# Two-layer attention trunk: value products for one head at a time, with the values' high and low halves side by side as stationary operand

## Chip, core and metric

The kernel runs on one core of one Trainium2 chip. The metric is device time in microseconds (us) for one execution. An engine here is TensorE (PE, its weight loads are PEld), VectorE (DVE), ScalarE (ACT), GpSimd (POOL) or the queue of SyncE (SP).

## What is computed

Two layers of a trunk over 544 tokens: 512 prompt tokens and 32 sample tokens that also see 1024 cached positions. The part that matters here:

```python
h = rmsnorm(x, g_pre_mix)
q, k, v, q_mla, ckv, k_rope, gate_a, gate_b = split(h @ w_in)
# branch A, 8 heads x 64, strictly causal, stick-breaking weights
z = einsum('bqhd,bkhd->bhqk', q, k) * SB_SCALE
a = where(visible, exp(log_sigmoid(z) + suffix_sum(log_sigmoid(-z))), 0)
o_sb = einsum('bhqk,bkhd->bqhd', a, v)
# branch B, 8 heads, latent attention, softmax over chunk-causal scores
p = softmax(where(visible, s, -inf));  o_mla = (p @ c_kv) @ w_uv
mix = (sigmoid(gate_a)*(o_sb @ w_proj_sb) + sigmoid(gate_b)*(o_mla @ w_proj_mla)) @ w_out
# then ConvFFN (w_up, causal conv, gelu, w_down) and a per-layer embedding
```

All is float32. A product of two float32 matrices is made as three products of rounded parts: each operand is split into a high part (fp32r) and a low part (what is left), and `PARTS = ((0,0),(0,1),(1,0))` multiplies high by high, high by low and low by high.

## The kernel before, in words

Activations lie transposed (features on partitions, 544 tokens in the free dimension). TensorE has a fixed, hand-written order. After a few opening projections each layer runs 37 **steps**, s = 0 to 36. Step s belongs to unit s: `("s", t, qb)` is query block qb (128 queries) of head pair t in branch A, `("m", t, qb)` the same in branch B, and S and M are units of the sample tokens. The order is: pairs s0, s1, unit S, pairs s2, s3, unit S, pairs m0 to m3, two units M. So a pair's four units start at step 0, 4, 9, 13, 18, 22, 26 and 30; this start is `start(br, t)`.

In step s TensorE does, in this order: scores of unit s (`sb_scores` L1610 and L1613, or `ml_scores` L1744 and L1750) into the PSUM banks 4 to 7; the tiles of `AHEAD` for this step (the value products `pv`, L1691 and L1695); `turn(s-1)`, which transposes the attention weights of the unit before (L1653, for samples L1643 and L1645); small tiles of `AFTER` (`vt`, `kv`, `ot` and others); and then from one to four quarters of projection tiles from `FILL` (L1536, twelve matmuls of 272 columns a quarter).

ScalarE and VectorE go through the same steps in their own fixed orders. ScalarE: sigmoids (L820, L825) or, after the scores' maxima, exponents (L839); evacuation of AHEAD tiles (L736); `weights_hi(s-1)` (L862); evacuation of AFTER and FILL tiles. VectorE: scans (L1231) or maxima (L1266, L1268); evacuation of AHEAD tiles; `weights_lo(s-1)`; `products(s)` (L1252) or `normalise(s)` (L1284), for which turn(s) waits; the rest. The scores of unit s wait until weights_lo(s-2) is done. All low parts go through one helper, `lo`, recorded as L1074.

Transposed weights of one pair lie in `at`, a single buffer. Before the change a pair's value products are two tiles: `pva` for query blocks 0 and 1 in step start+3, `pvb` for blocks 2 and 3 in step start+5. Each takes the values of both heads (128 columns) as stationary operand and the weights of both heads as moving one, so half of each output, where a head's values meet the other head's weights, is not read.

Tiles other than scores live in PSUM banks 0 to 3. A planner that runs when the program is built goes through the order of events, gives each tile one bank (`pv`, `ot`, `sv`, `zt`, ...) or a pair of banks (projections, `kv`, `vt`), and notes in `BEFORE` which tile had the bank last. `banks_free(t)` makes TensorE wait until the readers of that tile have counted up. For a value product the last reader is VectorE.

GpSimd splits each streamed weight chunk into its parts (L600, L606), in a ring of four slots; SP loads a chunk when the chunk four places before it has been used.

Of the kernel before, what the change touches and what calls it, by code (L numbers as in the profile page):

```python
# [110 lines left out]
def build(nc, x_in, p_in, wstream, vec, kc, vc, cct, cc, krc, consts, trig,  # L111
          y_out, k_out, v_out, c_out, kr_out, conv_out):
    top = ExitStack()
    with top:
# [59 lines left out]
        at = reg(b1, 2, 2, ATW)  # L174
# [3 lines left out]
        v_s = reg(b2, 2, 2, QB, P)  # L178
# [3 lines left out]
        vm = reg(b3, 2, 2, QB, P)  # L182
# [117 lines left out]
        AHEAD = {start(br, t) + d: [("pv" + h + br, t)] for br in "sm" for t in range(PAIRS) for h, d in (("a", 3), ("b", 5))}  # L300
# [124 lines left out]
        def released(c):  # L425
# [3 lines left out]
            if c in CACHES:  # L429
# [13 lines left out]
                 "z_done w_done b_done r_done a_done at_tr at_hi at_lo "  # L443
# [6 lines left out]
        with ExitStack() as st:  # L450
# [160 lines left out]
            def _(act):  # L611
# [16 lines left out]
                for layer in range(DEPTH):  # L628
# [101 lines left out]
                    def pv_tile(t):  # L730
                        act.wait_ge(S["p_done"], AT[t] + 1)
                        if t[0] == "pvas" and t[1] == 2:
                            act.wait_ge(pre["qr_in"], QR_MOVES * (layer + 1))
                        o, q = (o_sb if t[0][3] == "s" else o_ml), slice(0, SEQ // 2) if t[0][2] == "a" else slice(SEQ // 2, SEQ)
# [15 lines left out]
                    def kv_tile(t):  # L750
                        act.wait_ge(S["p_done"], AT[t] + 1)
                        ac(kn[:, t[1] % 2, 0], bank(t), ACT.Copy)
                        ac(vm[:, t[1] % 2, 0], bank(t, 1).rearrange("p (b l) -> p b l", l=P),
                           ACT.Copy).then_inc(S["act_read"], 1)
# [88 lines left out]
                    def weights_hi(n):  # L843
                        br, t, qb = units[n]
                        act.wait_ge(S["at_tr"], n + 1)
                        if br == "S":
                            act.wait_ge(S["p_done"], AT[("pvbs", 2 * t + 1)] + 1)
                            ac(aT_s[0:DEC, 0, PAST:PAST + P], bank(tail(n))[0:DEC, 0:P], ACT.Copy).then_inc(S["act_read"], 1)
                            ac(wide(aT_s[:, 0, 0:PAST]), z_view(n, 512), ACT.Copy).then_inc(S["at_hi"], 1)
                            return  # L850
                        if br == "M":
                            if t == 0:
                                act.wait_ge(S["p_done"], AT[("pvbm", PAIRS - 1)] + 1)
# [4 lines left out]
                        if qb == 0 and units[n - 1][0] == "S":  # L858
                            act.wait_ge(S["p_done"], AT[("sv", units[n - 1][1])] + 1)
                        elif t > 0 and qb in (0, 2):  # L860
                            act.wait_ge(S["p_done"], AT[(("pva" if qb == 0 else "pvb") + br, t - 1)] + 1)
                        ac(at_view(0, qb), z_view(n, P * (qb + 1)), ACT.Copy).then_inc(S["at_hi"], 1)  # L862
# [180 lines left out]
            def _(dve):  # L1043
# [17 lines left out]
                for layer in range(DEPTH):  # L1061
# [98 lines left out]
                    def vt_tile(t):  # L1160
                        dve.wait_ge(S["act_read"], aread(t))
                        lo(v_s[:, t[1] % 2, 1], bank(t).rearrange("p (b l) -> p b l", l=P), v_s[:, t[1] % 2, 0], None)
                        lo(v_tail[0:DEC, 1, t[1]], bank(t, 1)[0:DEC, 0:P], v_tail[0:DEC, 0, t[1]], "dve_read")

                    def pv_tile(t):
                        dve.wait_ge(S["act_read"], aread(t))
                        o, q = (o_sb if t[0][3] == "s" else o_ml), slice(0, SEQ // 2) if t[0][2] == "a" else slice(SEQ // 2, SEQ)
# [119 lines left out]
                    def weights_lo(n):  # L1287
# [207 lines left out]
            def _(pe):  # L1495
# [3 lines left out]
                for layer in range(DEPTH):  # L1499
# [135 lines left out]
                    def turn(n):  # L1635
# [443 lines left out]
```

## Time and profile before

| | |
|---|---|
| median of 3 runs | 1863.4 us (1861.43 to 1866.7) |
| the profiled execution, its own time | 1863.8 us |
| its span, first to last instruction | 1862.0 us |
| PE busy | 98% of the span |
| DVE, ACT, POOL busy | 49%, 30%, 58% |
| attention steps of layer 0 | about 43 to 310 us |
| attention steps of layer 1 | about 968 to 1235 us |

Busy time of PE is a union of pipelined matmuls, so the start of one matmul to the start of the next is the better measure of what one costs. "Idle" in a row is the engine's idle time just before the first instruction of that row, with what ended it.

### The profile page before, as it was taken

How to read it: one execution, taken by the hardware profiler on the slowest of the kernel's cores; microseconds unless marked ns; L12 is line 12 of the kernel's file. 1: busy time of each engine (PE TensorE's matmuls, PEld its weight loads, DVE VectorE, ACT ScalarE, POOL GpSimd, SP SyncE). 2: the span in 40 equal slices, each digit the busy share in tenths (PEclk: the TensorE clock that was granted, in tenths of full speed). 3: DMA queues.
4: the chain of work that ended last, by engine and by line, in shares of the span. 5: the costliest groups of instructions: out<-in, count | busy, mean ns of one | idle time of the engine just before them, and what ended most of it. 6: DMA issues, size and time to landing. Idle time of an engine off the chain costs nothing.

```text
span 1862.0 us, 33695 instructions
## 1 busy us (share of the span) xinstructions
PE 1832.2 (98%) x14262; PEld 1775.2 (95%) x14262; DVE 920.4 (49%) x1570; ACT 557.7 (30%) x1165; POOL 1073.5 (58%) x994
## 2 busy tenths in 40 slices
PE   9999999999999999999999999999999999999999
PEld 8989889999999999999999898899999999999999
DVE  6666675332755532523656666752237555225143
ACT  4434443112422221202334344431134222122021
POOL 8685534656555555556666854346465555555564
PEclk9999999999999999999999999999999999999999
DMA  5242111333222222223242421122422222222222
GB/s 187 87 130 75 64 41 59 112 99 133 69 91 89 82 91 91 87 78 100 95 146 89 126 74 58 48 78 86 142 94 69 91 84 87 91 91 82 84 88 94
DMA packets 76230, 170.48 MB, mean 92 GB/s; under 512 B 6384, under 2 KB 34160, under 8 KB 76080
## 3 DMA queue, kind: packets, MB, share of 16 engines
q1 hardware_dynamic: 68752, 160.79, 26.9%
q10 hardware_dynamic: 7328, 7.54, 1.3%
q8 instruction: 113, 1.85, 0.4%
q14 instruction: 37, 0.30, 0.0%
HBM read 156.41 MB, written 9.79 MB: 89 GB/s over the span
## 4 chain that ended last, share of the span: by engine, by line
PE 85%; DVE 6%; POOL 3%; ACT 3%; DMA 1%; issue 1%; SPq 0%; DVEq 0%; ACTq 0%; POOLq 0%
PE ps L1536 72%; PE ps L1571 2%; PE ps L1695 2%; POOL wsp L606 2%; PE ps L1653 2%; DVE xT L1408 1%; DVE xn L1074 1%; POOL wsp L600 1%; DVE mix L1405 1%; DVE R L1074 1%; DMA raw<-in_wstream 1%; ACT ps L839 1%; PE ps L1610 1%; PE ps L1744 1%; ACT R L862 1%
## 5 line engine op out<-in xcount | busy, mean ns | idle before, releaser
L1536 PE MATMUL ps<-xn,wsp 128*128 128x272 f32 x7824 | 1003.4, 289 | 9.2 <-POOL wsp L606 5.3
L1536 PEld LDWEIGHTS ps<-xn,wsp 128*128 128x128 f32 x7824 | 986.7, 189 | 13.2 <-issue 9.6
L606 POOL TENSOR_TENSOR wsp<-raw,wsp 128x256 fp32r<-128x256 f32 (+1 forms) x578 | 723.3, 1274 | 22.3
L600 POOL CAST wsp<-raw 128x512 fp32r<-128x512 f32 (+2 forms) x372 | 325.5, 890 | 662.4 <-DMA raw<-in_wstream 567.8
L1536 PE MATMUL ps<-R,wsp 128*128 128x272 f32 x3840 | 486.2, 288 | 0.1
L1536 PEld LDWEIGHTS ps<-R,wsp 128*128 128x128 f32 x3840 | 482.7, 189 | 1.3 <-DVE xT L1103 0.5
L1074 DVE SCALAR_TENSOR_TENSOR R<-ps,R 64x256 fp32r<-64x256 f32 (+8 forms) x232 | 127.8, 560 | 85.1 <-ACT R L674 27.9
L1424 DVE TENSOR_TENSOR mix<-ps,rstd 128x272 f32<-128x272 f32 x88 | 38.8, 441 | 202.6 <-PE ps L1536 192.2
L959 ACT ACTIVATE mix<-vv 128x2 f32<-128x2 f32 x88 | 17.9, 204 | 363.0 <-DVE mix L1426 363.0
L1074 DVE SCALAR_TENSOR_TENSOR R<-mix,R 128x544 fp32r<-128x544 f32 (+2 forms) x86 | 74.5, 867 | 81.3 <-ACT R L980 66.9
L1432 DVE SCALAR_TENSOR_TENSOR ps<-mix,vv,ps 128x546 f32<-128x546 f32 x88 | 69.4, 789 | 55.6 <-ACT ps L968 55.6
L1571 PE MATMUL ps<-xn,wsp 128*128 128x272 f32 x576 | 80.3, 295 | 6.8 <-DVE xn L1074 6.8
L1571 PEld LDWEIGHTS ps<-xn,wsp 128*128 128x128 f32 x576 | 74.5, 189 | 10.9 <-DVE xn L1074 9.8
L1471 DVE TENSOR_TENSOR A<-ps,A 128x544 f32<-128x544 f32 x32 | 23.2, 724 | 109.3 <-PE ps L1536 109.3
L1231 DVE TENSOR_TENSOR_SCAN xT<-xT 128x128 f32<-128x128 f32 (+3 forms) x64 | 62.1, 1011 | 20.2 <-ACT xT L820 20.2
L968 ACT ACTIVATE ps<-mix,vv 128x546 f32<-128x546 f32 x88 | 71.4, 812 | 1.6 <-DVE mix L1426 1.6
L1434 DVE SCALAR_TENSOR_TENSOR ps<-mix,vv,ps 128x546 f32<-128x546 f32 x88 | 69.6, 791 | 3.1
L1088 DVE TENSOR_TENSOR acc<-acc,mix 128x544 f32<-128x544 f32 x30 | 32.7, 1089 | 64.9 <-ACT mix L649 64.9
L862 ACT ACTIVATE R<-ps 128x256 fp32r<-128x256 f32 (+1 forms) x64 | 45.2, 707 | 46.9 <-PE ps L1653 46.2
L649 ACT ACTIVATE mix<-A 128x544 f32<-128x544 f32 x16 | 10.6, 661 | 150.4 <-DVE A L1471 150.4
L1695 PE MATMUL ps<-R 128*128 128x512 f32 x192 | 52.3, 407 | 0.6 <-issue 0.4
L1653 PE MATMUL ps<-con,xT 128*128 128x128 f32 x320 | 46.9, 277 | 4.2 <-DVE xT L1284 2.5
(228 smaller groups left out, 1441.3 us busy)
## 6 DMA issues: line engine op xcount, KB each, us to landing
raw<-in_wstream SPq DMA_DIRECT2D x233, 512.0 KB, 3.5
raw<-in_wstream SPq DMA_DIRECT2D x48, 128.0 KB, 2.6
raw<-in_wstream SPq DMA_DIRECT2D x16, 384.0 KB, 3.0
raw<-in_kc SPq DMA_DIRECT2D x8, 512.0 KB, 3.6
raw<-in_vc SPq DMA_DIRECT2D x8, 512.0 KB, 4.3
xT<-in_x_in SPq DMA_DIRECT2D x8, 272.0 KB, 4.8
out_k_out<-mix ACTq DMA_DIRECT2D x8, 272.0 KB, 2.9
xT<-in_x_in SPq DMA_DIRECT2D x1, 2176.0 KB, 9.3
```

Of the source, the lines that this page charges most:

```text
L600: ins = nc.gpsimd.tensor_copy(dst[:, 0, f], part[:, f])
L606: ins = nc.gpsimd.tensor_tensor(dst[:, 1, f], part[:, f], dst[:, 0, f].bitcast(F32), ALU.subtract)
L862: ac(at_view(0, qb), z_view(n, P * (qb + 1)), ACT.Copy).then_inc(S["at_hi"], 1)
L968: ac(uc[v], e[:, 0:T + 2], ACT.Identity, scale=vv[:, V_CW + f:V_CW + f + 1], bias=vv[:, V_CB + f:V_CB + f + 1]).then_inc(S["conv0"], 1)
L1074: ins = v.scalar_tensor_tensor(dst, src, scale, hi.bitcast(F32), ALU.mult, ALU.subtract)
L1231: v.tensor_tensor_scan(x, x, x, 1.0, ALU.mult, ALU.min).then_inc(S["r_done"], 1)
L1432: link(v.scalar_tensor_tensor(uc[w], uext[w][:, 1:T + 3], vv[:, V_CW + 2 * FT + f:V_CW + 2 * FT + f + 1], uc[w], ALU.mult, ALU.add))
L1434: v.scalar_tensor_tensor(uc[w], uext[w][:, 2:T + 4], vv[:, V_CW + 4 * FT + f:V_CW + 4 * FT + f + 1], uc[w], ALU.mult, ALU.add).then_inc(S[ ...
L1536: mm = pe.matmul(z[:, h], w[:, x, (k0 + k) * P:(k0 + k + 1) * P], rhs[:, y, k, h * HT:(h + 1) * HT], start=(k == 0 and (x, y) == (0, 0)), ...
L1571: mm = pe.matmul(z[:, h], w[:, x, k * P:(k + 1) * P], xn[:, y, k, h * HT:(h + 1) * HT], start=(k == 0 and (x, y) == (0, 0)), stop=(k == KT ...
L1653: mm = pe.transpose(ps[:, ZB + 2 * (n % 2) + r, kb * P:(kb + 1) * P], x[:, r, kb * P:(kb + 1) * P], ident)
L1695: mm = pe.matmul(z.rearrange("p r (b q) -> p r b q", b=2), val[:, x, kb], a[:, :, :, kb * P:(kb + 1) * P], start=(kb == 0 and i == 0), sto ...
```

## The change

Value products are made head by head. For head r of a pair the stationary operand is 64 columns of the values' high part beside 64 columns of the low part; the moving operand is the weights' high part and then their low part. One tile covers all four query blocks: key block kb meets the queries from block kb on, (4-kb)*128 columns. Rows 0 to 63 of the output are high values' products and rows 64 to 127 those of the low values; VectorE adds the halves when it evacuates. Both tiles of a pair, `pv0` and `pv1`, stand in step start+5; step start+3 has none. The weights' buffer and the values' buffers are laid out anew, transposes of head 0 are written in reversed block order, and head 1's output has its query blocks reversed until evacuation.

```diff
-        AHEAD = {start(br, t) + d: [("pv" + h + br, t)] for br in "sm" for t in range(PAIRS) for h, d in (("a", 3), ("b", 5))}
+        AHEAD = {start(br, t) + 5: [("pv0" + br, t), ("pv1" + br, t)] for br in "sm" for t in range(PAIRS)}
...
+        PV_AT = {t: n for n, t in enumerate([t for s in range(STEPS) for t in ahead(s) if t[0][0:2] == "pv"])}
...
         def at_view(x, qb):
-            o = qb * (qb + 1) // 2 * P
-            return at[:, x, :, o:o + P * (qb + 1)]
+            a = at[:, x, qb * P:(qb + 1) * P]
+            return bass.AP(tensor=a.tensor, offset=a.offset,
+                           ap=[a.ap[0], [(2 * ATW // P - 1 - 5 * qb) * P, 2], [3 * P, qb + 1], [1, P]])
+        def at_keys(x, r, kb):
+            o = (2 * ATW // P - 4 - 3 * kb if r else 4 * kb) * P
+            return at[:, x, o:o + (QB - kb) * P]
...
                     def pv_tile(t):                      # ScalarE
+                        r = int(t[0][2])
                         act.wait_ge(S["p_done"], AT[t] + 1)
-                        for r in range(2):
-                            ins = ac(o[64 * r:64 * r + 64, 0, t[1], q], bank(t)[64 * r:64 * r + 64, 256 * r:256 * r + 256], ACT.Copy)
-                        ins.then_inc(S["act_read"], 1)
+                        z = turned(bank(t)[0:64], r)
+                        o = (o_sb if t[0][3] == "s" else o_ml)[64 * r:64 * r + 64, 0, t[1], 0:SEQ]
+                        ac(turned(o, 0), z, ACT.Copy).then_inc(S["act_read"], 1)
...
                     def pv_tile(t):                      # VectorE
                         dve.wait_ge(S["act_read"], aread(t))
-                        for r in range(2):
-                            lo(o[64 * r:64 * r + 64, 1, t[1], q], bank(t)[64 * r:64 * r + 64, 256 * r:256 * r + 256],
-                               o[64 * r:64 * r + 64, 0, t[1], q], "dve_read" if r else None)
+                        r, z = int(t[0][2]), bank(t)
+                        o = (o_sb if t[0][3] == "s" else o_ml)[64 * r:64 * r + 64, :, t[1], 0:SEQ]
+                        lo(turned(o[:, 1], 0), turned(z[0:64], r), turned(o[:, 0], 0), "pv_low")
+                        dve.wait_ge(S["pv_low"], PV_AT[t] + 1)
+                        v.tensor_tensor(turned(o[:, 1], 0), turned(z[64:128], r), turned(o[:, 1], 0).bitcast(F32),
+                                        ALU.add).then_inc(S["dve_read"], 1)
...
-                            lo(at_view(1, qb), z_view(n, P * (qb + 1)), at_view(0, qb), "at_lo")
+                            v.tensor_tensor(at_view(1, qb), z_blocks(n, qb), at_view(0, qb).bitcast(F32), ALU.subtract).then_inc(S["at_lo"], 1)
...
                     def pv(t):                           # TensorE
-                        pe.wait_ge(S["at_lo"], n + 1)
-                        z, blocks = bank(t).rearrange("p (r q) -> p r q", r=2), 2 if t[0][2] == "a" else QB
-                        for kb in range(blocks):
-                            for i, (x, y) in enumerate(PARTS):
-                                if kb == blocks - 1:
-                                    mm = pe.matmul(z[:, :, P:2 * P], val[:, x, kb], at[:, y, :, o + 2 * kb * P:o + (2 * kb + 1) * P],
-                                                   start=False, stop=(i == 2))
-                                else:
-                                    a = at[:, y, :, o:o + 2 * (blocks - 1) * P].rearrange("p r (b q) -> p r b q", b=2)
-                                    mm = pe.matmul(z.rearrange("p r (b q) -> p r b q", b=2), val[:, x, kb],
-                                                   a[:, :, :, kb * P:(kb + 1) * P], start=(kb == 0 and i == 0), stop=False)
+                        if r == 0:
+                            pe.wait_ge(S["dve_read"], dread(("vt" if br == "s" else "kv", p)))
+                            pe.wait_ge(S["at_lo"], start(br, p) + QB)
+                        for kb in range(QB):
+                            w = (QB - kb) * P
+                            z = bank(t)[:, 0:w] if r else bank(t)[:, 512 - w:512]
+                            for x in range(2):
+                                mm = pe.matmul(z, val[:, 2 * kb + r].rearrange("p x f -> p (x f)"), at_keys(x, r, kb),
+                                               start=(kb == 0 and x == 0), stop=(kb == QB - 1 and x == 1))
                         mm.then_inc(S["p_done"], 1)
```

The planner's code is unchanged; its banks follow from the new order of tiles.

## Rows read from the trace of the kernel before

**Rows 1.** The page's busy times.
```profile
PE 1832.2 (98%) x14262; PEld 1775.2 (95%) x14262; DVE 920.4 (49%) x1570; ACT 557.7 (30%) x1165; POOL 1073.5 (58%) x994
```
**Rows 2.** TensorE in order of time, pair s0: start, length, what, count.
```profile
67.72 0.94 PE L1695 MATMUL ps<-R 128*128 128x512 f32 x3
...
68.85 0.82 PE L1653 MATMUL ps<-con,xT 128*128 128x128 f32 x6
...
75.56 1.09 PE L1653 MATMUL ps<-con,xT 128*128 128x128 f32 x8 [0.28 <-DVE xT L1252]
```
**Rows 3.** VectorE in order of time, step 3.
```profile
72.55 1.82 DVE L1074 SCALAR_TENSOR_TENSOR R<-ps,R 64x256 fp32r<-64x256 f32 x3
```
**Rows 4.** TensorE in order of time: runs of one size, 512 and 128 columns.
```profile
105.81 2.89 PE L1625 MATMUL ps<-wsp,R 128*128 128x512 f32 x12
...
208.25 1.45 PE L1718 MATMUL ps<-R 128*128 128x128 f32 x12
```
**Rows 5.** Groups by line and shape: busy us, mean ns, idle before.
```profile
L1456 DVE TENSOR_TENSOR mix<-mix,ps 128x512 f32<-128x512 f32 x44 | 30.3, 688 | 5.0 <-ACT mix L991 0.6
...
L1088 DVE TENSOR_TENSOR acc<-acc,mix 128x544 f32<-128x544 f32 x30 | 32.7, 1089 | 64.9 <-ACT mix L649 64.9
...
L1074 DVE SCALAR_TENSOR_TENSOR R<-ps,R 64x256 fp32r<-64x256 f32 x64 | 26.8, 418 | 25.1 <-ACT R L736 24.7
L1074 DVE SCALAR_TENSOR_TENSOR R<-ps,R 128x512 fp32r<-128x512 f32 x40 | 26.0, 679 | 1.0 <-ACT vtail L724 0.6 <-ACT R L753 0.5
...
L862 ACT ACTIVATE R<-ps 128x512 fp32r<-128x512 f32 x16 | 9.6, 599 | 18.0 <-PE ps L1653 18.0
```
**Rows 6.** TensorE in order of time, steps 9 and 10 of layer 0.
```profile
115.26 2.32 PE L1695 MATMUL ps<-R 128*128 128x512 f32 x9
...
117.77 0.27 PE L1643 MATMUL ps<-con,xT 128*32 128x128 f32 x1
...
118.67 6.25 PE L1536 MATMUL ps<-xn,wsp 128*128 128x272 f32 x48
```
**Rows 7.** VectorE in order of time, step 9.
```profile
119.08 1.77 DVE L1231 TENSOR_TENSOR_SCAN xT<-xT 128x128 f32<-128x128 f32 x2
```
**Rows 8.** GpSimd in order of time, from step 8 of layer 0.
```profile
110.30 3.23 POOL L600 CAST wsp<-raw 128x512 fp32r<-128x512 f32 x2 [4.88 <-DMA raw<-in_wstream]
```
**Rows 9.** TensorE in order of time, step 10 of layer 0.
```profile
131.45 3.75 PE L1536 MATMUL ps<-xn,wsp 128*128 128x272 f32 x28 [1.92 <-POOL wsp L606]
```
**Rows 10.** TensorE in order of time, step 10 of layer 1.
```profile
1055.64 4.52 PE L1536 MATMUL ps<-xn,wsp 128*128 128x272 f32 x23 [2.16 <-POOL wsp L606]
```
**Rows 11.** Busy time by stretch there; the number before the DMA share is the granted clock.
```profile
1054.00:1056.00 2.00, 0.36 (x1) 0.39 (x2) 1.89 (x3) 0.00 (x0) 2.00 (x4) 0.84 0.91 228
```
**Rows 12.** TensorE and VectorE in order of time, step 14.
```profile
160.60 2.30 PE L1695 MATMUL ps<-R 128*128 128x512 f32 x9
...
161.56 1.27 DVE L1231 TENSOR_TENSOR_SCAN xT<-xT 128x256 f32<-128x256 f32 x2 [1.62 <-ACT xT L820]
```
**Rows 13.** TensorE, ScalarE and VectorE in order of time, step 25 and the turn after.
```profile
243.32 1.09 PE L1653 MATMUL ps<-con,xT 128*128 128x128 f32 x8 [0.50 <-DVE xT L1284]
...
240.00 0.75 ACT L839 ACTIVATE ps<-ps,small,rtok 128x512 f32<-128x512 f32 x1
...
238.78 0.23 DVE L1268 TENSOR_SCALAR small<-small,rtok 128x2 f32<-128x2 f32 x1
```
**Rows 14.** TensorE and VectorE in order of time, steps 27 and 28.
```profile
247.68 2.30 PE L1695 MATMUL ps<-R 128*128 128x512 f32 x9
...
252.55 0.62 PE L1744 MATMUL ps<-R,Ar 64*128 64x384 f32 x4 [0.49 <-DVE R L1074]
...
251.18 1.31 DVE L1074 SCALAR_TENSOR_TENSOR R<-ps,R 64x256 fp32r<-64x256 f32 x3 [2.28 <-ACT R L736]
```
**Rows 15.** TensorE in order of time, step 35.
```profile
298.53 2.31 PE L1695 MATMUL ps<-R 128*128 128x512 f32 x9
...
302.99 6.24 PE L1536 MATMUL ps<-xn,wsp 128*128 128x272 f32 x48 [0.81 <-ACT R L854]
```

More of the change, by code:

```diff
@@ L173, in build @@
         ATW = 10 * P
-        at = reg(b1, 2, 2, ATW)
+        at = reg(b1, 2, 2 * ATW)
         aT_s = reg(b1, 2, (CB + 1) * P)
@@ L177, in build @@
         b2 = b1 + 4 * ATW
-        v_s = reg(b2, 2, 2, QB, P)
+        v_s = reg(b2, 2, 2 * QB, 2, 64)
         kn = reg(b2, 2, 2, SEQ)
@@ L181, in build @@
         q_smp = reg(b3 + 2 * PAIRS * P, 2, PAIRS, P)
-        vm = reg(b3, 2, 2, QB, P)
+        vm = reg(b3, 2, 2 * QB, 2, 64)
         ol_s = reg(b3, 2, 2 * P)
@@ L239, in z_view, with z_blocks @@
             return ps[:, ZB + 2 * (n % 2):ZB + 2 * (n % 2) + 2, 0:w]
+        def z_blocks(n, qb):
+            return z_view(n, P * (qb + 1)).rearrange("p r (b q) -> p r b q", q=P)
         def bt_view(n, w):
@@ L254, in at_view, with turned, v_parts @@
         def at_view(x, qb):
-            o = qb * (qb + 1) // 2 * P
-            return at[:, x, :, o:o + P * (qb + 1)]
+            a = at[:, x, qb * P:(qb + 1) * P]
[4 more added lines that the diff above has]
+            return at[:, x, o:o + (QB - kb) * P]
+        def turned(ap, r):
+            z = ap.rearrange("p (b q) -> p b q", q=P)
+            return z[:, ::-1] if r else z
+        def v_parts(buf, i, y):
+            return buf[:, i, :, y]
         def backward(ap, n):
@@ L730, in pv_tile @@
                     def pv_tile(t):
+                        if t[0] == "pv0s" and t[1] == 2:
+                            act.wait_ge(pre["qr_in"], QR_MOVES * (layer + 1))
+                        r = int(t[0][2])
                         act.wait_ge(S["p_done"], AT[t] + 1)
-                        if t[0] == "pvas" and t[1] == 2:
-                            act.wait_ge(pre["qr_in"], QR_MOVES * (layer + 1))
-                        o, q = (o_sb if t[0][3] == "s" else o_ml), slice(0, SEQ // 2) if t[0][2] == "a" else slice(SEQ // 2, SEQ)
-                        for r in range(2):
-                            ins = ac(o[64 * r:64 * r + 64, 0, t[1], q], bank(t)[64 * r:64 * r + 64, 256 * r:256 * r + 256], ACT.Copy)
-                        ins.then_inc(S["act_read"], 1)
+                        z = turned(bank(t)[0:64], r)
+                        o = (o_sb if t[0][3] == "s" else o_ml)[64 * r:64 * r + 64, 0, t[1], 0:SEQ]
+                        ac(turned(o, 0), z, ACT.Copy).then_inc(S["act_read"], 1)
                     def qn_tile(t):
@@ L752, in kv_tile @@
                         ac(kn[:, t[1] % 2, 0], bank(t), ACT.Copy)
-                        ac(vm[:, t[1] % 2, 0], bank(t, 1).rearrange("p (b l) -> p b l", l=P),
+                        ac(v_parts(vm, t[1] % 2, 0), bank(t, 1).rearrange("p (b f) -> p b f", f=64),
                            ACT.Copy).then_inc(S["act_read"], 1)
@@ L859, in weights_hi @@
                             act.wait_ge(S["p_done"], AT[("sv", units[n - 1][1])] + 1)
-                        elif t > 0 and qb in (0, 2):
-                            act.wait_ge(S["p_done"], AT[(("pva" if qb == 0 else "pvb") + br, t - 1)] + 1)
-                        ac(at_view(0, qb), z_view(n, P * (qb + 1)), ACT.Copy).then_inc(S["at_hi"], 1)
+                        elif t > 0 and qb == 0:
+                            act.wait_ge(S["p_done"], AT[("pv1" + br, t - 1)] + 1)
+                        ac(at_view(0, qb), z_blocks(n, qb), ACT.Copy).then_inc(S["at_hi"], 1)
                     if layer > 0:
@@ L1161, in vt_tile @@
                         dve.wait_ge(S["act_read"], aread(t))
-                        lo(v_s[:, t[1] % 2, 1], bank(t).rearrange("p (b l) -> p b l", l=P), v_s[:, t[1] % 2, 0], None)
+                        lo(v_parts(v_s, t[1] % 2, 1), bank(t).rearrange("p (b f) -> p b f", f=64), v_parts(v_s, t[1] % 2, 0), None)
                         lo(v_tail[0:DEC, 1, t[1]], bank(t, 1)[0:DEC, 0:P], v_tail[0:DEC, 0, t[1]], "dve_read")
@@ L1178, in kv_tile @@
                         lo(kn[:, t[1] % 2, 1], bank(t), kn[:, t[1] % 2, 0], None)
-                        lo(vm[:, t[1] % 2, 1], bank(t, 1).rearrange("p (b l) -> p b l", l=P), vm[:, t[1] % 2, 0], "dve_read")
+                        lo(v_parts(vm, t[1] % 2, 1), bank(t, 1).rearrange("p (b f) -> p b f", f=64), v_parts(vm, t[1] % 2, 0), "dve_read")
                     def ql_tile(t):
@@ L1652, in turn @@
                             for kb in range(qb + 1):
-                                mm = pe.transpose(ps[:, ZB + 2 * (n % 2) + r, kb * P:(kb + 1) * P], x[:, r, kb * P:(kb + 1) * P], ident)
+                                j = qb - kb if r else kb
+                                mm = pe.transpose(ps[:, ZB + 2 * (n % 2) + r, j * P:(j + 1) * P], x[:, r, kb * P:(kb + 1) * P], ident)
                         mm.then_inc(S["at_tr"], 1)
```

15 lines of the change are left out of this document (6 added, 9 removed).

## The prediction

> **What bounds the kernel now.** I read the page first: PE is busy 98% of the span, the other engines at most 58% [rows 1]. So time leaves only if TensorE has less to do, or if a wait of TensorE goes or comes. Then TensorE's waits, and its order of time through the attention steps of layer 0: projection quarters cover most turns, and the stalls are 0.3 to 0.5 us each, at turns that come too early for VectorE [rows 2, 13, 14], one of 0.81 us for a PSUM bank [rows 15], and one for GpSimd's weights, 1.92 us in layer 0 at 131.45 us and 2.16 us in layer 1 [rows 9, 10]. Last I read ScalarE's and VectorE's order of time in each step that holds a value product, because these engines free the banks.
>
> **Matmul prices.** A matmul costs what lies from its start to the next one's. pva (three of 512 columns, three of 256) takes 68.85 - 67.72 = 1.13 us [rows 2]; pvb (nine and three) takes 117.77 - 115.26 = 2.51 [rows 6]. The six more make 1.38 us: 0.23 for 512. 272 columns are at most 6.25 / 48 = 0.13 [rows 6], so 256 some 0.12, and 0.08 is left for a group's start. 128 columns: nine transposes in 118.67 - 117.77 = 0.90 us, 0.10 to 0.11 [rows 6]; runs of twelve, with the tail of the last in them, give 0.24 and 0.12 as upper ends for 512 and 128 [rows 4]. No row shows 384 columns with 128 rows: between 0.12 and 0.23; halfway, 0.175, since from 256 to 512 the cost follows the columns.
>
> **What TensorE saves.** Before, a pair costs pva 68.85 - 67.72 = 1.13 us in step start+3 [rows 2] and pvb 2.51 us in step start+5. After, each head has two matmuls each of 512, 384, 256 and 128 columns: 0.46 + 0.35 + 0.24 + 0.21 = 1.26 us, so both 2.52, with the start 2.60 us (2.4 to 2.8 by the bounds for 384). All of this stands in start+5. So start+3 loses 1.13 us, start+5 gains 0.10. Over 16 pairs (4 pairs, 2 branches, 2 layers) that is 16.5 us, if nothing waits.
>
> **Start+3, does all of it count?** Turn(start+2) can come 1.13 us earlier: its weights come from the step before, and nothing stalls there. The next turn, start+3, stands in step start+4:
> - s0 and s2: it already waits 0.28 us for VectorE [rows 2], whose chain begins with scans after the k tile. That chain holds pva's two evacuations (the row of three has them and weights_lo), 2 * 0.418 less overlap = 0.8 us [rows 3, 5]. So 0.85 saved.
> - s1, s3, m3: a sample unit follows with long scores, no stall: 1.13 each.
> - m0 to m2: the turn waits for normalise, that for exponents, those for the maxima, whose end is 239.01 in step 25; exponents start at 240.00 after pva's evacuation and weights_hi [rows 13]. They can start 0.95 earlier, no more. So 0.97, 1.0, and 1.2 for m0, where a small bank wait goes too.
>
> Sum per layer: 2 * 0.85 + 3 * 1.13 + 3.17 = 8.3 us. Less 8 * 0.10 = 0.8.
>
> **What evacuation costs.** ScalarE: one copy of 512 a tile, 0.60 us. VectorE: `lo` 0.68 and an add of PSUM and SBUF 0.69 [rows 5], 1.39 a tile with the wait between; 64 partitions cost as much as 128, only the free size counts (a 64x256 `lo` takes 0.418 as above). Nothing shows an add whose halves and result lie on different partitions: from 0.69, as this add without a shift, up to 1.09, as the kernel's dearest add, of 544, both from SBUF [rows 5]; I take 0.69, the row with one operand in PSUM. Nor is the copy with a shift of partitions shown; 0.60 to 0.75, taken 0.60. With T as the start of pv0: pv0 is complete at T+1.5 and copied at T+2.15; pv1 complete at T+2.8 and copied at T+3.4. VectorE, free at F, gives pv0 back at max(F, T+2.15) + 1.4 and pv1 1.35 later. Before, one tile came back 1.5 us after its end. The subtraction in weights_lo costs the same as `lo`.
>
> **Banks: what TensorE now waits for.** I worked the planner's rule through the new order of tiles. In four steps the tile that TensorE opens right after the pair's turn gets a bank of pv0 or pv1, and waits for VectorE's adds:
> - Step 9 (s1): v3 opens banks 2 and 3, the last of them pv1's. Before, it opened 0 and 1 and didn't wait: turn(8) ends and L1536 starts at 118.67 [rows 6]. VectorE first has the rotation of qr1 and scans(9) until 119.08 + 1.77 = 120.85 [rows 7]. Then four instructions, 2.7 us: pv1 is free at 123.55. TensorE is there at T + 2.6 + 0.9 = 118.77. Stall 4.8 us. It replaces the stall of 1.92 (2.16) us that GpSimd causes one step later: GpSimd's unbroken run begins at 110.30 with a load [rows 8] that a tile of step 7 releases, so it isn't moved by the new stall. Net 2.9 us a layer.
> - Step 14 (s2): `ot` 0 gets pv0's bank. T is 160.60; VectorE's scans end at 162.83 [rows 12]; free at 164.25. TensorE is there at T + 2.6 + 0.2. Stall 0.8.
> - Step 18 (s3): ga1 gets pv1's bank. VectorE is idle when pv0 comes; free at T + 2.15 + 2.75 = T + 4.9; TensorE there at T + 3.5. Stall 1.4.
> - Step 35 (m3): gb3 gets both, free at T + 4.9 = 303.45 instead of 302.99, where it already stalls [rows 15]. 0.5.
>
> Elsewhere there is cover: in step 5, q2 opens 3.3 us after the pair's end, free 0.6 us before; in m0 to m2 the next user comes a step later. But in m1 and m2, steps 27 and 31, a single quarter covers VectorE: weights_lo ends at T + 5.2 instead of 251.18 + 1.31 = T + 4.8, and scores(28), which already waits 0.49 us for it [rows 14], goes with it: 0.3 less the 0.1 counted, 0.16 each, 0.3.
>
> VectorE loses nothing else: step 3, 7, 12 and 16 get lighter by 0.8 us each.
>
> Sum of waits per layer: 2.9 + 0.8 + 1.4 + 0.5 + 0.3 = 5.9 us.
>
> **The clock.** In layer 1 the granted clock fell behind TensorE's 2.16 us of idleness, to 0.84 in the mean of a 2 us stretch [rows 11], so to its lower level, 1.2 GHz, for part of it; the 23 matmuls that follow take 4.52 us, against 23 * 0.13 = 3.0 at the full 2.4 GHz [rows 6, 10]: 1.4 to 1.6 us. In layer 0 it didn't fall. A stall of 4.8 us in both layers should bring it both times, once more than before: 1.6 us.
>
> **Sum.** Per layer 8.3 - 0.8 - 5.9 = 1.6 saved, 3.2 for both, less 1.6 for the clock: 1.6. The profiled execution takes 1863.8 us (span 1862.0), so 1862.2; the runs' median is 0.4 below: **1861.8 us**.
>
> **Rivals.**
> - *A, no bank waits:* the banks come free in time (the planner gives others, or VectorE does the evacuation ahead of its scans). Then 8.3 - 0.8 - 0.3 = 7.2 a layer, 14.4: **1849 us**. For it: TensorE's own work does shrink by 16.5. Against: VectorE's order puts scans first [rows 7].
> - *B, half of the waits:* some of the four are covered, above all step 9: 1855 us.
> - *C, the add is dear (the other side):* at 1.09 us and not 0.69, each of pv0 and pv1 comes back 0.4 later. Step 9 loses 0.8, 14 0.4, 18 and 35 0.8 each, 27 and 31 0.8 each, step 5 a little: 4.6 a layer, 9.2 more: **1871 us**. It is slower by over 0.3% from an add of 1.0 us on. For it: nothing shows this shift of partitions. Against: adds of PSUM and SBUF take 0.69 in 44 cases [rows 5].
> - *D, wide matmuls don't pay by column:* if only the number of matmuls counted, 16 instead of 18 at 0.107, a pair would save 0.2 us and not 1.04: 13 us more, **1875 us**. Against: 512 columns cost 0.23 us and 128 about half of that [rows 4, 6]. A page speaks for a mild form of D: the Trainium skill, "TensorE: Matmul & The Clock Gate", section "Back-to-back issue gap", gives about 131 ns for 512 columns and 81 ns for 128 in a stream of weight loads and matmuls. By it a pair would fall from about 2.16 to 1.70 us, an estimate from that page, so the sum would be some 9 us higher than mine. The trace disagrees: 0.23 and 0.10 us.
>
> **Chances and range.** My forecast 0.62 (its own range 1857 to 1866: each of ten stalls is off by some tenths), A 0.14, B 0.10, C 0.11, D 0.03. A measurement of this kernel can tell 0.3%, 5.6 us. Faster than 1857.8: A, most of B, and a tenth of my case: 0.28. Slower than 1869.0: C, D: 0.12. Within: 0.60. The range, 1850 to 1869, leaves out D, most of C and half of A.
>
> **What would show it.** L1695 and L1691 become one line with 256 matmuls, about 2.6 us a pair; no value product in steps 3, 7, 12, 16; VectorE's `lo` of 64x512 and an add after it, 0.7 us each, 32 of each; an idle time of 4.8 us before L1536 in step 9, ended by VectorE's add, and none, or little, for GpSimd in step 10; 0.8 before `ot`, 1.4 before ga1, 1.3 before gb3; a lower clock behind step 9 in both layers. I am wrong if the stall in step 9 is short, if the add isn't 0.7, or if waits show up that I called covered (q2 in step 5, scores in steps 23 and 24).

## The result

The changed kernel takes 1866.7 us (median of 18 runs, 1864.4 to 1868.0) against 1862.6 for the kernel before, run beside it (18 runs, 1859.2 to 1866.7). The ratio is 1.0023, 95% interval 1.0016 to 1.003: a small loss, below 0.3% but measurable, where 1.6 us of gain was forecast. The profiled execution takes 1866.0 us.

The traces below are of one execution each, and executions differ in how long TensorE's clock is low: the changed kernel has a mean granted clock of 0.995 to 0.997 in all 18, while the kernel before has 0.997 to 1.000 in the 43 that stand beside the experiments, at 1859.4 to 1868.5 us. Its profiled execution, from which the forecast started, had one such stretch in its steps, in layer 1.

### The profile page after: what moved, and what is told of

It is laid out like the page before. It is cut to its first block, busy times and chain, and to the rows that moved or that the text cites. A ratio compares the mean times of both kernels' runs of the same rounds, so it can differ in the third digit from the quotient of the medians.

```text
span 1864.2 us, 33587 instructions
## 1 busy us (share of the span) xinstructions
PE 1817.8 (98%) x14230; PEld 1765.7 (95%) x14230; DVE 932.1 (50%) x1570; ACT 553.7 (30%) x1133; POOL 1071.3 (57%) x994
## 3 DMA queue, kind: packets, MB, share of 16 engines
q8 instruction: 113, 1.85, 0.4%
## 4 chain that ended last, share of the span: by engine, by line
PE 88%; DVE 7%; ACT 2%; issue 2%; POOL 1%; DMA 0%; SPq 0%; DVEq 0%; ACTq 0%; POOLq 0%
PE ps L1559 74%; PE ps L1594 2%; PE ps L1714 2%; PE ps L1677 2%; DVE xn L1095 1%; DVE xT L1431 1%; DVE mix L1428 1%; PE ps L1633 1%; ACT ps L860 1%; DVE R L1325 1%; PE ps L1763 1%; PE ps L1696 1%; PE ps L1648 1%; DVE xT L1254 1%; PE ps L1769 1%
## 5 line engine op out<-in xcount | busy, mean ns | idle before, releaser
L1559 PE MATMUL ps<-xn,wsp 128*128 128x272 f32 x7824 | 1006.6, 289 | 19.2 <-issue 18.2
L1559 PEld LDWEIGHTS ps<-xn,wsp 128*128 128x128 f32 x7824 | 989.1, 189 | 23.9 <-issue 21.4
L621 POOL CAST wsp<-raw 128x512 fp32r<-128x512 f32 (+2 forms) x372 | 318.5, 871 | 671.3 <-DMA raw<-in_wstream 578.7
L1559 PE MATMUL ps<-R,wsp 128*128 128x272 f32 x3840 | 486.2, 288 | 0.1
L1559 PEld LDWEIGHTS ps<-R,wsp 128*128 128x128 f32 x3840 | 482.7, 189 | 1.2 <-DVE xT L1124 0.5
L1095 DVE SCALAR_TENSOR_TENSOR R<-mix,R 128x544 fp32r<-128x544 f32 (+2 forms) x86 | 71.0, 826 | 81.9 <-ACT R L1001 66.9
L1095 DVE SCALAR_TENSOR_TENSOR R<-ps,R 64x512 fp32r<-64x512 f32 (+8 forms) x136 | 71.0, 534 | 44.2 <-ACT R L695 23.4
L1325 DVE TENSOR_TENSOR R<-ps,R 128x256 fp32r<-128x256 f32 (+1 forms) x64 | 52.0, 812 | 17.6 <-ACT R L883 17.3
```

The costliest lines, as they stand in the source:

```text
L621: ins = nc.gpsimd.tensor_copy(dst[:, 0, f], part[:, f])
L1095: ins = v.scalar_tensor_tensor(dst, src, scale, hi.bitcast(F32), ALU.mult, ALU.subtract)
L1325: v.tensor_tensor(at_view(1, qb), z_blocks(n, qb), at_view(0, qb).bitcast(F32), ALU.subtract).then_inc(S["at_lo"], 1)
L1559: mm = pe.matmul(z[:, h], w[:, x, (k0 + k) * P:(k0 + k + 1) * P], rhs[:, y, k, h * HT:(h + 1) * HT], start=(k == 0 and (x, y) == (0, 0)), ...
```

## The profile after

The page, busy times, in the columns of [rows 1]:

```profile
PE 1817.8 (98%) x14230; PEld 1765.7 (95%) x14230; DVE 932.1 (50%) x1570; ACT 553.7 (30%) x1133; POOL 1071.3 (57%) x994
```

TensorE's waits, in total, times, longest:

```profile
PE ps L1559 <- issue: 18.2, 12, 5.5
...
PE ps L1763 <- DVE R L1325: 5.5, 10, 1.0
PE ps L1677 <- DVE xT L1307: 4.5, 6, 0.9
```

L1559 is the projections' line (L1536 before). "issue" means that the profile names no releaser. The projections' bank waits behind a pair show so; the engines' order of time shows which instruction ends each. Four of the twelve, 0.40 us each, stand in the kernel before as well. TensorE, step 9 of layer 0, to be laid beside [rows 6]:

```profile
114.03 2.75 PE L1714 MATMUL ps<-R 128*128 128x512 f32 x16
116.62 0.27 PE L1666 MATMUL ps<-con,xT 128*32 128x128 f32 x1
116.73 1.04 PE L1668 MATMUL ps<-con,xT 128*128 128x128 f32 x8
123.26 8.04 PE L1559 MATMUL ps<-xn,wsp 128*128 128x272 f32 x48 [5.50 <-issue]
```

The pair's 16 matmuls take 116.62 - 114.03 = 2.59 us. Then v3 waits 5.50 us. The same row in layer 1:

```profile
1048.18 5.08 PE L1559 MATMUL ps<-xn,wsp 128*128 128x272 f32 x24 [4.76 <-issue]
```

VectorE, the stretch of layer 0, to be laid beside [rows 7]:

```profile
116.44 1.14 DVE L1167 TENSOR_TENSOR mix<-mix 128x544 f32<-128x544 f32 x1
117.62 1.13 DVE L1168 TENSOR_TENSOR mix<-mix 128x544 f32<-128x544 f32 x1
118.67 1.74 DVE L1254 TENSOR_TENSOR_SCAN xT<-xT 128x128 f32<-128x128 f32 x2
120.33 0.66 DVE L1095 SCALAR_TENSOR_TENSOR R<-ps,R 64x512 fp32r<-64x512 f32 x1
121.02 0.69 DVE L1192 TENSOR_TENSOR R<-ps,R 64x512 fp32r<-64x512 f32 x1
121.75 0.69 DVE L1095 SCALAR_TENSOR_TENSOR R<-ps,R 64x512 fp32r<-64x512 f32 x1
122.47 0.69 DVE L1192 TENSOR_TENSOR R<-ps,R 64x512 fp32r<-64x512 f32 x1
```

L1167 and L1168 are the last two of the three arithmetic instructions that rotate qr1, L1095 is `lo`, L1192 the add of halves. The last add ends at 123.16 and TensorE goes on at 123.26. The stretches behind the wait, and the same place in layer 1 (the number before the DMA share is the granted clock):

```profile
120.43:127.26 6.83, 4.00 (x18) 4.03 (x19) 4.37 (x7) 0.01 (x1) 6.67 (x11) 0.50 0.01 2
127.30:131.30 4.00, 4.00 (x34) 3.85 (x33) 0.00 (x0) 0.00 (x0) 0.94 (x2) 1.00 0.00 0
1045.44:1052.27 6.83, 4.09 (x18) 4.12 (x19) 4.28 (x7) 0.65 (x2) 6.67 (x11) 0.50 0.00 0
```

TensorE stands idle from 117.8, the clock falls to 1.2 GHz at 120.43 and is back at 127.26. Of the 6.83 us, 4 are work at half speed: v3's 48 matmuls take 8.04 us, not 6.25. The other places, TensorE: step 5, `ot` in step 14, ga1 in step 18, gb3 in step 35 [rows 15], and the scores of step 28 [rows 14]:

```profile
87.24 1.74 PE L1559 MATMUL ps<-xn,wsp 128*128 128x272 f32 x12 [0.42 <-issue]
...
167.61 0.41 PE L1807 MATMUL ps<-con,acc 128*128 128x128 f32 x2 [0.72 <-ACT R L758]
...
199.79 2.50 PE L1559 MATMUL ps<-xn,wsp 128*128 128x272 f32 x18 [1.36 <-issue]
...
256.35 0.62 PE L1763 MATMUL ps<-R,Ar 64*128 64x384 f32 x4 [1.01 <-DVE R L1325]
...
305.69 1.49 PE L1559 MATMUL ps<-xn,wsp 128*128 128x272 f32 x10 [1.37 <-issue]
```

The starts of the steps' scores, laid beside those of the kernel before, give what each step of layer 0 gained or lost. Predicted values in brackets:

| place | us |
|---|---|
| the eight steps without pva, less what the next turn waits longer | 8.7 - 1.1 = +7.6 (+8.3) |
| the pairs' longer matmuls, seven up to step 35 | -0.6 (-0.7) |
| q2 in step 5, bank | -0.64 (0) |
| step 9, stall 5.5, clock 1.8, rest 0.2 | -7.5 (-4.8 - 1.6 = -6.4) |
| step 10, GpSimd's stall gone | +2.2 (+1.9) |
| step 14, `ot` | -1.0 (-0.8) |
| step 18, ga1 | -1.6 (-1.4) |
| scores of steps 28 and 32 | -0.7 (-0.3) |
| all other steps | +0.1 (0) |
| sum, up to step 35 | -2.1 (+0.6) |

With gb3's longer wait, 0.6, layer 0 has lost 2.7 us by 471 us. Between there and the steps of layer 1 the changed kernel wins 1.0 us back, 0.8 of it because a wait for GpSimd at 961 us in the kernel before is missing; no experiment looked at that place. Layer 1's steps lose 0.6: the terms are those of layer 0, but step 9 loses 6.9, and step 10 gains 3.8, because the kernel before had a clock drop there as well. The two profiled executions are 2.2 us apart, the medians 4.1.

## Experiments: each part of the change alone

The first four kernels ran on one chip, where the kernel before had a median of 1863.2 us.

**The move alone.** The kernel before, with pva moved into step start+5, in front of pvb.

```diff
-        AHEAD = {start(br, t) + d: [("pv" + h + br, t)] for br in "sm" for t in range(PAIRS) for h, d in (("a", 3), ("b", 5))}
+        AHEAD = {start(br, t) + 5: [("pva" + br, t), ("pvb" + br, t)] for br in "sm" for t in range(PAIRS)}
```

> The kernel before, with pva moved to step start+5 ahead of pvb: the move alone, with the old products and the old evacuation. The planner then gives the same banks as in the changed kernel. Theory W: TensorE's work is unchanged, VectorE has 1.6 us for a pair and not 2.8; stall before v3 in step 9 about 3.3 us (GpSimd's 2 us goes for it), ga1 0.6, gb3 1, so 3 to 6 us slower than before: 1865 to 1868, ratio 1.002 to 1.003. Rival M (the place costs nothing, only the dearer evacuation does): ratio 1.000 within 0.0005.

Measured: 1871.5 us, ratio 1.0046 [1.0032, 1.006], 8.3 us slower where 3 to 6 were expected. The profiled execution is the fastest of the five, 1869.0 us. Each pva costs in its new step what it saved in the old one (about 1.0), so what is left are waits. Step 9, TensorE:

```profile
118.39 1.03 PE L1645 MATMUL ps<-con,xT 128*128 128x128 f32 x8
122.53 3.75 PE L1536 MATMUL ps<-xn,wsp 128*128 128x272 f32 x28 [3.10 <-issue]
```

VectorE starts the pair's four low parts (64x256, 0.39 to 0.43 us each) at 120.70, behind the rotation and the scans, and ends them at 122.43. In layer 1 TensorE waits 3.46 us there, and the clock falls. So step 9 stalls when both tiles of a pair stand together in it, also without an add. ga1 and gb3 wait 0.82 each.

**No add.** The changed kernel without L1192: rows 64 to 127 of each value tile (the low values' products) are not added, and `lo` is VectorE's last reader.

```diff
-                        lo(turned(o[:, 1], 0), turned(z[0:64], r), turned(o[:, 0], 0), "pv_low")
-                        dve.wait_ge(S["pv_low"], PV_AT[t] + 1)
-                        v.tensor_tensor(turned(o[:, 1], 0), turned(z[64:128], r), turned(o[:, 1], 0).bitcast(F32),
-                                        ALU.add).then_inc(S["dve_read"], 1)
+                        lo(turned(o[:, 1], 0), turned(z[0:64], r), turned(o[:, 0], 0), "dve_read")
```

> The changed kernel without VectorE's add of the two halves (the output lacks the products of the values' low part). 0.72 us less for each tile on VectorE. Theory W: each tile that waits for pv0 waits 0.7 less and each that waits for pv1 1.4 less: step 9 stall 4.1 (3.4), ot 0, ga1 about 0, gb3 0.4, scores behind steps 27 and 31 0.4 instead of 1.0, q2 0. About 6 us a layer, 12 in all: 1854 to 1857, ratio 0.995 to 0.997. Rival D: VectorE isn't the bound, its evacuation is hidden, 1866 to 1867, same as the changed kernel.

Measured: 1854.6 us, ratio 0.9954 [0.9942, 0.9967], 12 us under the changed kernel, as expected. In layer 0 the stall of step 9 is shorter by two adds and a little:

```profile
121.44 2.77 PE L1556 MATMUL ps<-xn,wsp 128*128 128x272 f32 x11 [3.85 <-issue]
```

In layer 1 it is 4.02 us for 4.76, shorter by one add only (3.4 was expected). `ot` doesn't wait, ga1 and gb3 wait 0.5, the scores of step 28 0.1; the turn in that step then waits 0.3.

**ScalarE alone gives the banks back.** VectorE's two instructions are replaced by a memset of the output's low half, so the low part and the low values' products are both left out. The copy on ScalarE stays.

```diff
-            return (1, 0) if t[0] in ACT_ONLY or t[0] == "down" else (1, 1)
+            return (1, 0) if t[0] in ACT_ONLY or t[0] == "down" or t[0][0:2] == "pv" else (1, 1)
...
+                        v.memset(o[:, 1].bitcast(F32), 0.0)
```

> The changed kernel, with VectorE's two instructions for each tile replaced by a memset of the low half (the output lacks the low part of the attention results), so that ScalarE's copy alone gives the bank back. Theory W: banks come back at T + 3.4, before TensorE asks; the whole saving of 16 us less some stalls of the chains shows, GpSimd's stall of 2 us is back: 1847 to 1851, ratio 0.992 to 0.994. Rival D: at most 2 us better than before, ratio 0.999 or more.

Measured: 1842.5 us, ratio 0.989 [0.9877, 0.9904], 4.5 us under the lower end of what was expected. TensorE in step 9, and at the head of step 10:

```profile
116.25 1.04 PE L1665 MATMUL ps<-con,xT 128*128 128x128 f32 x8
117.04 6.27 PE L1556 MATMUL ps<-xn,wsp 128*128 128x272 f32 x48
...
128.75 3.50 PE L1556 MATMUL ps<-xn,wsp 128*128 128x272 f32 x26 [0.83 <-POOL wsp L627]
```

No value product's bank is waited for any more, GpSimd's stall is shorter than before (0.83 for 1.92), and the clock doesn't fall in any step. So the matmuls' saving is real: 20.7 us under the kernel before. Sixteen pairs at 1.07 (1.14 + 2.51 - 2.58, the medians of all pairs) make 17.1; GpSimd's shorter stall, twice about 1.0, and the clock drop that the kernel before has in layer 1, 1.8, make the rest. gb3's wait is gone as well (0.8 a layer), and the turns behind start+3 wait longer (1.0 a layer), which about cancels. This kernel is what rival A described, and the loss of the real one against it, 24 us, is what VectorE's evacuation of the pairs costs, clock drops included.

The three medians add up. The move alone costs 8.3 us, the new products without the add are 16.9 us faster than that, about the matmuls' 17.1, and the adds cost 12.1: in sum 3.5 us more than the kernel before, where 4.1 were measured.

**VectorE's rotations later.** In the changed kernel VectorE rotates qr0 and qr1 one step later, behind `products`.

```diff
+                        for t, i in fills(s - 1) if s > 0 else []:
+                            if t[0] == "qr" and i == 3:
+                                evacuate(t)
-                        for t in (after(s) if s >= NS else []) + [t for t, i in fills(s) if i == 3]:
+                        for t in (after(s) if s >= NS else []) + [t for t, i in fills(s) if i == 3 and t[0] != "qr"]:
                             evacuate(t)
```

> The changed kernel, with the rotations of qr0 and qr1 put one step later on VectorE (behind the products of step 5 and step 9), so that VectorE is free for the value products' evacuation. Theory W (waits for banks that VectorE gives back late eat the saving): in step 9 pv1 comes back at about T + 5.3 us and TensorE is there at T + 3.6, so the stall before v3 falls from 5.5 (4.8 in layer 1) to about 1.7 us, the clock no longer falls behind it, GpSimd's stall in step 10 comes back with up to 0.5 us, and q2 in step 5 waits no more. 8 to 9.5 us less than the changed kernel: about 1857 to 1859, ratio to before 0.997 to 0.998. Rival D (columns don't pay, the saving was never there): no more than the stalls that the profile shows can go, and TensorE's sum of value products would be as before; the same 1867 if the time reappears as GpSimd's stall.

Measured: 1863.5 us, ratio 1.0002 [0.9994, 1.0011]: a miss of 4 to 6 us. Step 9 went as expected, the wait is 1.35 us, and q2 doesn't wait in step 5. But the edit also moves qr0, in front of step 6, where the value turn and the quarter of k2 behind q2's last one now wait:

```profile
91.71 0.74 PE L1726 MATMUL ps<-con,mix 128*128 128x128 f32 x5 [1.60 <-DVE mix L1124]
92.20 4.75 PE L1562 MATMUL ps<-xn,wsp 128*128 128x272 f32 x36
98.80 1.37 PE L1562 MATMUL ps<-xn,wsp 128*128 128x272 f32 x9 [1.85 <-ACT R L695]
...
122.83 5.37 PE L1562 MATMUL ps<-xn,wsp 128*128 128x272 f32 x41 [1.35 <-issue]
```

Against the changed kernel step 9 is 6.0 us shorter in layer 0 and 5.1 in layer 1, and step 6 is 3.9 and 4.6 longer, so most of what step 9 gives is lost in step 6.

## Experiments: can the waits be taken away?

The next three ran on one chip, the kernel before at 1863.0 us.

**Only qr1's rotation later.** This leaves qr0 where it is.

```diff
-                        for t in (after(s) if s >= NS else []) + [t for t, i in fills(s) if i == 3]:
+                        if s > 0 and (("qr", 1), 3) in fills(s - 1):
+                            evacuate(("qr", 1))
+                        for t in (after(s) if s >= NS else []) + [t for t, i in fills(s) if i == 3 and t != ("qr", 1)]:
                             evacuate(t)
```

> The changed kernel, with one edit: of VectorE's rotations only the later tile's (qr1) is put off by a step, behind the products of step 9, so that the pass of step 9 finds VectorE free; the first tile's rotation stays where the change has it, since putting off both made the value turn and the q2 projection wait in steps 5 and 6. Theory (the loss sits in banks that VectorE gives back late, above all in step 9): the stall at the head of v3 in step 9 falls from 5.5 and 4.8 us to about 1.4 in both layers, the clock no longer drops behind it (about 1.8 us each time), and steps 5 and 6 keep the times of the changed kernel; some 11 us less than the changed kernel, near 1855.7 us, ratio to the kernel before 0.9965. Rival (the work put off only moves the wait to step 10 or 11, as it did with both tiles): no better than 1863, ratio 1.000, with a new VectorE wait in step 10 to 12 of 3 us or more.

Measured: 1855.7 us, ratio 0.996 [0.9948, 0.9972], 11 us under the changed kernel, as expected. VectorE and TensorE in step 9:

```profile
118.94 0.69 DVE L1192 TENSOR_TENSOR R<-ps,R 64x512 fp32r<-64x512 f32 x1
...
122.14 0.98 DVE L1166 TENSOR_TENSOR mix<-mix 128x544 f32<-128x544 f32 x1
123.15 1.14 DVE L1167 TENSOR_TENSOR mix<-mix 128x544 f32<-128x544 f32 x1
```

```profile
119.73 6.24 PE L1561 MATMUL ps<-xn,wsp 128*128 128x272 f32 x48 [1.35 <-issue]
```

The last add ends at 119.63, the rotation follows it. The waits in steps 9 of both layers shrink by 7.5 us together, and two clock drops of 1.8 us go; that is the 11 us. This kernel beats both.

**And `ot` later.** In the same kernel the turn of the first normalised tile stands behind step 16, not 14.

```diff
-        AFTER = { ... 13: [("ukt", 0)], 14: [("ot", 0)],
+        AFTER = { ... 13: [("ukt", 0)], 16: [("ot", 0)],
```

> The kernel with the later rotation of one tile, and one more edit: the turn of the first normalised tile is put off from behind step 14 to behind step 16. Theory: the turn's wait of 0.7 us and the wait it leaves in its step go, about 1 us a layer, near 1853.7 us, ratio 0.9953, and 2 us under the kernel without this edit. Rival (the normalisation is only late there because VectorE has a backlog, which the next pass then meets): the wait reappears at the next bank in steps 15 to 17, no difference over 0.5 us.

Measured: 1855.3 us, ratio 0.9956 [0.9944, 0.9968], the same. The wait of 0.72 us before `ot` is gone and another stands in step 16, in the middle of the projections:

```profile
173.66 0.38 PE L1809 MATMUL ps<-con,acc 128*128 128x128 f32 x2
173.80 3.25 PE L1561 MATMUL ps<-xn,wsp 128*128 128x272 f32 x24
178.01 1.74 PE L1561 MATMUL ps<-xn,wsp 128*128 128x272 f32 x12 [0.96 <-issue]
```

The rival was right in what it forecast: no difference over 0.5 us. `ot` takes a bank in step 16 now, and the planner gives others to the tiles behind it.

**And q2's bank later.** In that kernel step 5 gets two quarters and step 6 five, so q2 opens in step 6.

```diff
-                      [4, 4, 4, 3, 3, 3, 4, 4, ...
+                      [4, 4, 4, 3, 3, 2, 5, 4, ...
```

> The kernel with both edits before, and one more: of the projections' matmuls dealt out to steps 5 and 6, one unit more goes to step 6, so that the q2 projection opens its bank in step 6, behind the pass of step 5. Theory: the 0.42 us that q2 waits in step 5 goes and step 5 loses no time against the kernel before, 0.5 to 0.7 us a layer, near 1852.5 us, ratio 0.9947. Rival (TensorE has then less to do in step 5 and waits for the weights or the products instead, and q2's rotation is late for step 9): the same time or up to 2 us more, with a new wait in step 5 or 9.

Measured: 1856.5 us, ratio 0.9962 [0.9949, 0.9974], no better. q2's wait (0.48 us in layer 1 of the kernel without this edit, 0.2 in layer 0) is replaced by one of the scores behind it, for weights_lo, which VectorE does behind the same four instructions:

```profile
87.44 0.80 PE L1635 MATMUL ps<-R 64*128 64x384 f32 x6 [0.39 <-DVE R L1325]
```

**The late rotation in the kernel before.** The edit of the first of these kernels, in the kernel before (its median here 1863.5 us).

> The kernel before the change, with VectorE's rotation of qr1 put off by a step, the edit that took 11 us from the changed kernel. Theory (the edit helps the changed kernel only because it gives back a bank that the change made v3 wait for): here v3's banks don't come from the pair, TensorE's waits of 0.4 us or so stay where they are and GpSimd's 1.92 us in step 10 too, so the time is the same within 1 us, ratio 0.9995 to 1.0005, and the 7.3 us by which the changed kernel with this edit is ahead belong to the change. Rival (the rotation is early in the kernel before as well and the edit is a gain of its own): 3 us or more less, ratio 0.998 or lower.

Measured: 1860.2 us, ratio 0.9984 [0.9974, 0.9995]: the rival was right, the edit is worth 3.3 us by itself. The gain is in step 10, 1.7 us in layer 0 and 3.3 in layer 1, where GpSimd's stall falls to 0.23 us (0.21 in layer 1, without a clock drop):

```profile
130.27 6.26 PE L1538 MATMUL ps<-xn,wsp 128*128 128x272 f32 x48 [0.23 <-POOL wsp L606]
```

The rotation doesn't touch GpSimd's data; why it matters stands in the last section. The profiled executions are 4.7 us apart and the medians 3.3; how the 3.3 divide between the stall and the clock isn't shown. With the same edit on both sides the change is worth 1860.2 - 1855.7 = 4.5 us (from two chips, 0.996 / 0.9984 = 0.9976; by the two intervals, from about 1.5 to 7.5 us).

## Why the prediction missed

The forecast was 1861.8 us and the kernel took 1866.7, inside the range but with the sign of the difference wrong. Of the 4.9 us, 3.8 lie in the sum (1866.0 for the profiled execution against 1862.2), and 1.1 in how profiled executions stand to their medians. The mechanism was right, and nearly every wait came out longer than its term. Of the shortfall in the profiled execution, both layers together, step 9 has 1.6 us, q2 in step 5 1.4, the turns behind start+3 1.3, and the scores of steps 28 and 32 0.8; the 1.0 us won between the layers, which no term held, hid part of it.

- **What TensorE saves: right.** A pair takes 2.57 to 2.61 us, predicted 2.60. The 384-column price, chosen halfway at 0.175, measures 0.175. Start+3 gave 8.7 a layer before the waits of the next turns, and the kernel in which nothing waits for a value bank shows the whole saving.
- **The add and the copy: right.** `lo` 0.68, add 0.694, copy 0.59. An add whose operands and result lie on different partitions costs as much as one where they don't; rival C falls. Rival D falls too: from start to start 512 columns take 0.231 us, 256 0.118 and 128 0.11.
- **Step 9: right mechanism, too small.** Predicted 4.8 us, measured 5.50 and 4.76. The term took VectorE's scans to end at 120.85 with the pair at 115.26, 5.6 us after T. They ended at 120.33 with the pair at 114.03 (118.67 + 1.74 less the overlap of the next), 6.3 us after. TensorE came 1.2 us earlier, VectorE only 0.5: its three rotation instructions took 1.10, 1.14 and 1.13 us, against 0.73, 1.02 and 1.02 before. The error is in F, the time at which VectorE comes free, which the prediction took from the kernel before. Time saved ahead of a stall that another engine ends is given back in it, and the sum had booked it as kept.
- **GpSimd's stall: right.** It is gone, +2.2 for +1.9. The scores of steps 23 and 24, named as a sign of being wrong, wait no longer than before.
- **`ot`, ga1, gb3: right.** 0.72, 1.36 and 1.37 for 0.8, 1.4 and 1.3.
- **The step that failed: "Elsewhere there is cover".** q2 in step 5 was said to find its bank free 0.6 us before it needs it. It waits 0.42, and the step loses 0.64 beside the pair's 0.1 (0.46 and 0.73 in layer 1). VectorE's last add ends at 87.14, which is T + 6.3, because it comes free of its scans only at T + 3.5:

```profile
79.13 0.94 DVE L1166 TENSOR_TENSOR mix<-mix 128x544 f32<-128x544 f32 x1
80.11 1.14 DVE L1167 TENSOR_TENSOR mix<-mix 128x544 f32<-128x544 f32 x1
81.28 1.02 DVE L1168 TENSOR_TENSOR mix<-mix 128x544 f32<-128x544 f32 x1
82.22 2.17 DVE L1254 TENSOR_TENSOR_SCAN xT<-xT 128x256 f32<-128x256 f32 x2
```

  In the kernel before the same three instructions took 0.82, 0.72 and 0.72, and the scans 1.65, and VectorE then idled 0.9 us until ScalarE's copy of pvb. The prediction had VectorE free of them at T + 2.6, 0.9 us sooner, as in the kernel before. GpSimd lay otherwise beside them. Before the change it idled for 1.56 us, beside most of the three; in the changed kernel for 0.21 us only. GpSimd before and after:

```profile
81.83 1.96 POOL L600 CAST wsp<-raw 128x512 fp32r<-128x512 f32 x2 [1.56 <-DMA raw<-in_kc]
```

```profile
80.87 1.90 POOL L621 CAST wsp<-raw 128x512 fp32r<-128x512 f32 x2 [0.21 <-DMA raw<-in_kc]
```

  So the step that failed is that VectorE's instructions would take the time in the changed kernel that they took before. What VectorE's slower instructions have to do with GpSimd stands in the last section; that it is the whole of the delay here is read from these rows and not tested. The experiment that moved q2 shows that the delay isn't the bank's alone: weights_lo is as late.
- **Pairs m0 to m2: too small.** The turns of steps 22, 26 and 30 wait 0.88, 0.64 and 0.73 us, for 0.27, 0.50 and 0.50 before, so that start+3 keeps 7.6 and not 8.3 in layer 0; the scores of steps 28 and 32 wait 1.01, 0.5 each more than before, and lose 0.7 together for 0.3 predicted. The scores' extra wait is the adds': without them it is 0.1. The turns' isn't: they wait 0.74, 0.64 and 0.71 in layer 0 without the adds, and 0.47, 0.64 and 0.72 with the move alone. Why m0's start+3 keeps 0.7 of the 1.2 us predicted stays open.
- **The clock: right in count, short in price.** One drop more than before was forecast, and the profiled executions have two against one. Each costs 1.8 us of TensorE time, predicted 1.6.

By layers: predicted 0 for layer 0 and +1.6 for layer 1, measured -2.7 and -0.6, with +1.0 between the two. No experiment separated the clock's share in step 9 from the stall's; the price of 1.8 us is read from v3's matmuls.

## What to carry to other kernels

When work is merged to save the bound engine's time, look at who frees its outputs: here 17 us of matmuls were bought with 32 adds and wider low parts on an engine that is half idle on average, but had a queue just where the bank was wanted. A stall that another engine ends swallows whatever was saved ahead of it, so price it by the moment at which that engine comes free in the changed kernel, and rebuild its order of time at each place instead of using one delay for all. A duration read in the kernel before is good only while what runs beside it stays the same. Then move that engine's unhurried work (a rotation needed a step later) behind the release; moving TensorE's own tiles only moved the wait.

## What the runs showed of the hardware

**VectorE and GpSimd slow each other down** when VectorE's operands all lie in SBUF. A rotation instruction (128x544, both inputs in SBUF) takes 0.72 or 0.73 us while GpSimd is idle and up to 1.15 beside it. VectorE, the kernel with both rotations late, step 6, where GpSimd is idle until 90.47:

```profile
88.68 0.73 DVE L1166 TENSOR_TENSOR mix<-mix 128x544 f32<-128x544 f32 x1
89.44 0.72 DVE L1167 TENSOR_TENSOR mix<-mix 128x544 f32<-128x544 f32 x1
90.20 0.73 DVE L1168 TENSOR_TENSOR mix<-mix 128x544 f32<-128x544 f32 x1
```

GpSimd, the kernel before with the late rotation: four TENSOR_TENSOR beside almost no SBUF-only work of VectorE (the end of a scan, 0.2 us), and four of which the last two run beside the rotation.

```profile
117.80 2.82 POOL L606 TENSOR_TENSOR wsp<-raw,wsp 128x256 fp32r<-128x256 f32 x4
120.56 1.18 POOL L600 CAST wsp<-raw 128x512 fp32r<-128x512 f32 x2
121.82 3.80 POOL L606 TENSOR_TENSOR wsp<-raw,wsp 128x256 fp32r<-128x256 f32 x4
```

Those two take 1.2 us each, the others 0.74. `lo` and the adds, which read PSUM, leave GpSimd at 2.8 us for four. GpSimd's unbroken run up to the weights of step 10 took 20.95 us before (110.30 to 131.25) and 19.59 with the rotation moved (110.47 to 130.06): fewer of its instructions fell beside rotations and scans. This is why VectorE's order moves a stall that GpSimd causes. That this explains the 3.3 us is a reading of the two traces, not a separate experiment. The Trainium skill, "SBUF — State Buffer", section "SBUF: two separate sides", describes a port pair that these two engines share as an exclusive lock, held for a whole instruction, and names VectorE operations with two inputs in SBUF among those that take it. The trace agrees in which instructions are slowed: the rotation's 0.73 and 1.14 us, and `lo`, which reads PSUM and leaves GpSimd alone. Whether the added time is a lock being waited for, these rows can't show.

**TensorE's clock doesn't fall behind every idle time, and the length of the idle time alone doesn't say behind which.** At 1.2 GHz for 3.4 us: behind an idle time of 2.16 us (before, layer 1), 3.46 (the move alone, layer 1), 3.85 (no add, layer 0), 1.85 (both rotations late, layer 1), and 1.99 and 2.05 at about 1800 us (no add; `ot` later). For 6.8 us: behind 4.02 (no add, layer 1), 4.76 and 5.50. None behind 1.92 (before, layer 0), 3.10 (the move alone, layer 0), 1.35, and 1.85 in layer 0 of the kernel with both rotations late, where layer 1 had a fall at the same place behind the same wait. What decides it stays open.
